# Expert matrices fetched as one 16 KB piece per partition, and the two halves of the down product computed side by side

## The reference, cut to what matters

```
def expert_block(args):
    xe, e = args
    return (jax.nn.silu(xe @ w_gate[e]) * (xe @ w_up[e])) @ w_down[e]
...
'w_gate': nrm(ks[16], (DEPTH, N_EXPERTS, d, f), d ** -0.5),      # d = 1024, f = 512
'w_up': nrm(ks[17], (DEPTH, N_EXPERTS, d, f), d ** -0.5),
'w_down': nrm(ks[18], (DEPTH, N_EXPERTS, f, d), f ** -0.5),
```

## Time and profile before

| | |
|---|---|
| median of 3 runs | 2983.72 us (2981.38 to 2986.08) |
| the profiled execution, its own time | 2976.64 us |
| its span, first to last instruction | 2974.8 us |
| PE busy | 2399.9 us, 81% |
| DVE busy | 1747.3 us, 59% |
| ACT busy | 1194.0 us, 40% |
| mean granted TensorE clock | 0.891 of full speed |
| expert stage of layer 0, of layer 1 | about 1548 to 2087 us, about 2399 to 2941 us of the span |

### The profile page before, as it was taken

How to read it: one execution, slowest core, us unless ns; L and a number is a source line. 1 busy time by engine, 2 the same in 40 slices (tenths; PEclk the granted TensorE clock), 3 DMA queues, 4 the chain that set the end, 5 groups by cost and what they waited for, 6 DMA issues and landing times. The chain is left out here.

```text
span 2974.8 us, 30862 instructions
## 1 busy us (share of the span) xinstructions
PE 2399.9 (81%) x11408; PEld 1674.4 (56%) x11408; DVE 1747.3 (59%) x2142; ACT 1194.0 (40%) x1399; POOL 347.7 (12%) x431
## 2 busy tenths in 40 slices
PE   5779789996798998877739999999267569999995
PEld 4557677875676776644625555554155445555552
DVE  3646545445473545476347767776547357777674
ACT  2223244332232442244026566565214146566662
POOL 0100000100000001000122111121110122111211
PEclk9879999997898998888759999999579679999997
DMA  8235465550545643500349999998610479999993
GB/s 294 86 124 205 141 197 179 177 198 29 207 165 171 212 173 126 143 1 1 128 172 367 384 389 384 384 385 301 208 28 1 151 246 387 389 390 385 382 380 145
DMA packets 315905, 655.44 MB, mean 220 GB/s; under 512 B 18192, under 2 KB 63840, under 8 KB 315040
## 3 DMA queue, kind: packets, MB, share of 16 engines
q1 hardware_dynamic: 296272, 612.13, 57.6%
q0 software_dynamic: 18288, 38.72, 4.1%
q10 hardware_dynamic: 1248, 3.25, 0.3%
HBM read 653.70 MB, written 21.31 MB: 227 GB/s over the span
## 5 line engine op out<-in xcount | busy, mean ns | idle before, releaser
L554 PE MATMUL bank<-sb_ring_rounded,sb_hT_rounded 128*128 128x512 f32 x2864 | 767.4, 404 | 38.8 <-DVE sb_ring_rounded L1486 11.3
L554 PEld LDWEIGHTS bank<-sb_ring_rounded,sb_hT_rounded 128*128 128x128 f32 x2864 | 554.2, 195 | 163.4 <-issue 14.7
L1486 DVE TENSOR_TENSOR sb_ring_rounded<-sb_ring,sb_ring_rounded 128x2048 fp32r<-128x2048 f32 (+1 forms) x150 | 332.7, 2259 | 242.0 <-ACT sb_ring_rounded L1103 241.7
L1022 PE MATMUL bank<-sb_ring,sb_arena 128*64 128x512 f32 x1024 | 453.1, 595 | 1.8 <-DVE sb_arena L2044 1.8
L2035 DVE TENSOR_TENSOR sb_ring_rounded<-sb_ring,sb_hT_rounded 128x2048 fp32r<-128x2048 f32 x128 | 287.6, 2288 | 247.2 <-ACT sb_hT_rounded L1362 245.5
L1103 ACT ACTIVATE sb_ring_rounded<-sb_ring 128x2048 fp32r<-128x2048 f32 (+1 forms) x150 | 275.2, 1884 | 325.8 <-PE bank L554 146.7
L1000 PE MATMUL bank<-sb_ring_rounded,sb_arena_rounded 128*128 128x512 f32 x1024 | 405.2, 396 | 0.0
L554 PE MATMUL bank<-sb_ring_rounded,sb_arena_rounded 128*128 128x512 f32 x976 | 299.4, 394 | 2.0 <-DVE sb_arena_rounded L1474 1.0
L1022 PEld LDWEIGHTS bank<-sb_ring,sb_arena 128*64 128x64 f32 x1024 | 135.0, 137 | 268.6 <-issue 264.5
L1362 ACT ACTIVATE sb_hT_rounded<-sb_ring 128x2048 fp32r<-128x2048 f32 x128 | 237.3, 1901 | 84.2 <-DMA sb_ring<-in_w_gate 84.2
L1000 PE MATMUL bank<-sb_hT_rounded,sb_arena_rounded 128*128 128x512 f32 x512 | 212.8, 416 | 68.4 <-DVE sb_arena_rounded L2039 68.4
(11 more groups left out here) (292 smaller groups left out, 2847.3 us busy)
## 6 DMA issues: line engine op xcount, KB each, us to landing
sb_ring<-in_w_gate SPq DMA_DIRECT2D x64, 2048.0 KB, 20.2
sb_ring<-in_w_up SPq DMA_DIRECT2D x64, 2048.0 KB, 23.2
sb_ring<-in_w_down SPq DMA_DIRECT2D x64, 2048.0 KB, 20.3
sb_ring<-in_w_ada SPq DMA_DIRECT2D x48, 1024.0 KB, 8.4
sb_ring<-in_ffn_w_gu SPq DMA_DIRECT2D x44, 1024.0 KB, 7.9
sb_ring<-in_xa_w_kv SPq DMA_DIRECT2D x16, 1024.0 KB, 10.8
sb_ring<-in_ffn_w_down SPq DMA_DIRECT2D x16, 1024.0 KB, 6.6
sb_ring<-in_od_w_in SPq DMA_DIRECT2D x12, 1024.0 KB, 8.7
```

Of the source, the lines that this page charges most:

```text
L554: ins = pe.matmul(bank[b][0:rows, :], rnd(x), rnd(w[:, k, :]), start=start and k == k0 and q == 0, stop=stop and k == k1 - 1 and q == len( ...
L1022: ins = pe.matmul(bank[S0 + n][0:ROWS, :], mactT[:, j, k, :], w[:, k, n * NB:(n + 1) * NB], start=k == 0, stop=k == 3)
L1486: dve.tensor_tensor(rnd(w), w, whole(high_of(n)[:, k0:k1, :]), ALU.subtract).then_inc(*c.up(s["w_lo"]))
```

## The change

The fetches, the two groups of transposes and the down product change together. A partition p of a gate or up slot held rows p, 128+p, 256+p and so on of the matrix, eight pieces of 2 KB; of a down slot, rows p, 128+p, 256+p and 384+p, four pieces of 4 KB. Now it holds rows 8p to 8p+7 (of the down matrix 4p to 4p+3), which lie side by side in DRAM. To match, the transposes take every 8th column of the tokens from k on (every 4th of the activations), where they took 128 adjacent ones. The down product alternates between its halves, and the hi half goes to PSUM partitions 64 to 127.

```
-                    src = src.rearrange("o (k p) n -> p (o k) n", p=P)
+                    src = src.rearrange("o (p k) n -> p (o k) n", p=P)
...
-                        ins = pe.transpose(bank[T0 + j][:, k * ROWS:(k + 1) * ROWS], mx[0:ROWS, j, k * P:(k + 1) * P], ident[0:ROWS, 0:ROWS])
+                        ins = pe.transpose(bank[T0 + j][:, k * ROWS:(k + 1) * ROWS], mx[0:ROWS, j, k:D:KD], ident[0:ROWS, 0:ROWS])
...
-                        ins = pe.transpose(bank[2 * j][:, k * ROWS:(k + 1) * ROWS], mact[0:ROWS, j, k * P:(k + 1) * P], ident[0:ROWS, 0:ROWS])
+                        ins = pe.transpose(bank[2 * j][:, k * ROWS:(k + 1) * ROWS], mact[0:ROWS, j, k:EXP_H:4], ident[0:ROWS, 0:ROWS])
...
-                    for n, part in enumerate(("lo", "hi")):
-
+
+                    for part in ("lo", "hi"):
                         since(pe, m[f"y_{part}"], e)
-                        for k in range(4):
-                            ins = pe.matmul(bank[S0 + n][0:ROWS, :], mactT[:, j, k, :], w[:, k, n * NB:(n + 1) * NB], start=k == 0, stop=k == 3)
-                        ins.then_inc(m[f"pe_y_{part}"], 1)
+                    for k in range(4):
+                        for n, part in enumerate(("lo", "hi")):
+                            ins = pe.matmul(bank[S0 + n][n * ROWS:(n + 1) * ROWS, :], mactT[:, j, k, :], w[:, k, n * NB:(n + 1) * NB],
+                                            start=k == 0, stop=k == 3)
+                            if k == 3:
+                                ins.then_inc(m[f"pe_y_{part}"], 1)
...
-                    dve.tensor_copy(my[0:ROWS, j, NB:2 * NB], bank[S1][0:ROWS, :]).then_inc(m["y_hi"], 1)
+                    dve.tensor_copy(my[0:ROWS, j, NB:2 * NB], bank[S1][ROWS:P, :]).then_inc(m["y_hi"], 1)
```

## The result

The changed kernel takes 2909.88 us (median of 4 runs, 2906.74 to 2913.15), the kernel before 2984.05 us (4 runs, 2981.38 to 2986.08). The ratio is 0.9752, with a 95% interval of 0.9735 to 0.9769: 74 us less, where 92 were forecast.

The account below looks back on a forecast made before the run. The DMA queue was taken to bound the expert steps, with other loops close behind. Savings of 45 + 40 us in the layers' steps and 13 at the ends, 98, less 6 given back, made 92: 2892 us, range 2868 to 2932.

Parts of the forecast that it names:

- What bound the kernel before: Expert stages: the DMA queue ends last in each step, 17.05 us in layer 0 and 16.68 us in layer 1.
- The cross-check: ACT's waits for the gate matrix, 46 + 38 us, plus 13 us at the layers' ends: 97 us.
- Part 1, the rate: Expert fetches in 16 KB pieces: 428 GB/s, steps of 15.3 and 15.0 us, saving 45 + 40 us with the floor.
- the 6 us given back: Expert steps: 0.1 us a step subtracted from the saving, for two loops within 0.3 us tied by six slots.
- Part 2: Down product's halves side by side: 3.24 us less a product, on the path only at layer ends, 13 us in all.
- Part 3: Twelve stepped transposes a step: costed at nothing, covered by PE's 2.7 us of slack and 0.48 us free at the four.
- the doubling: Stepped transposes: at most twice as long, 0.12 us each, and hidden; a rival with slow ones, 0.43 us, had 4%.
- The floor: Loop of DVE and ACT in an expert step: 15.0 us, which the change doesn't shorten.
- The clock rival: PE's clock falls in one step of six, 3.4 us each: 34 us back, 2926 us; chance 6%.
- The rivals of the rate: Expert transfers stay at 385 GB/s: 2971 us, 6%; or 16 KB pieces fall to 350 GB/s: 3085 us, 5%.
- of the overlap: Rival: no overlap in the down product, PE's chain of 15.77 us is the step; saves 53, 2931 us; 7%.
- the prediction's price for each packet: DMA transfers: 0.018 us for each packet plus 0.0358 us a KB, so 0.604 us for a 16 KB piece.

Follow-up runs that it names:

- e4: The kernel before with three quarters of the gate and up work left out, all transfers kept in 2 and 4 KB pieces: 2956.71 us.
- e2: The kernel before with only the down product side by side, fetches and transposes unchanged: 2964.17 us, ratio 0.9957.
- e3: The changed kernel with three quarters of the gate and up work left out, all transfers kept in long pieces: 2872.06 us.
- e5: The changed kernel with two float32 matmuls, read by nobody, in PE's wait for DVE after each down product: 2905.2 us, ratio 0.976.
- e12: e5 with POOL's gathers and scatters cut to 8 of 64 rows, all work on the matrices still done: 2873.01 us.
- e1: The kernel before with only the new fetch layout and stepped transposes, down product unchanged: 2952.04 us, ratio 0.9908.
- e8: The changed kernel with each expert matrix fetched by two transfers of 8 KB pieces: 2909.8 us, ratio 0.9767.

## Why the prediction was right, and where it was off

Sign, mechanism and range were right: 2909.88 us lies within 2868 to 2932. Point by point:

- **What bound the kernel before.** Right: with three quarters of the gate and up work gone, the short pieces still gave 382 GB/s (e4), and the side by side product alone didn't shorten the steps (e2). The cross-check (46 + 38 + 13 = 97 us) came near by luck: it left out ACT's waits for the up matrix, as long again, 42.9 us in layer 0 and 34.6 in layer 1:

```profile
ACT sb_hb_rounded L1362 <- DMA sb_ring<-in_w_up: 42.9, 25, 2.7
```

- **Part 1, the rate.** This is the term that was mis-sized. "The cautious end is the rate really seen, 428 GB/s" gave steps of 15.3 and 15.0 us. Measured are 408 and 412 GB/s in the stages, and 412 and 416 with little other work (e3). With the prediction's own bytes that is 6.55 / 0.408 = 16.05 and 6.43 / 0.412 = 15.6 us; the steps came out at 15.91 and 15.54. The queue's packets came to 27 a step and engine (10757 in 400 us), where the prediction counted 24. The 428 had been read in 8 us of one queue that had the engines to itself, and was carried over to 500 us of matrices with POOL's rows beside them. The steps gave 45 - 27.0 = 18 us less than the sum had in layer 0 and 40 - 28.5 = 11.5 us less in layer 1, 29.5 in all; of the 11.5, up to 5 may be the clock's dips (e5). Against it stand the 6 us given back for two loops close to each other, which were not on top of that, and 1.4 us more at the ends and elsewhere: 92 - 29.5 + 6 + 1.4 = 69.9 us.
- **Part 2.** Right. Sixteen records take 3.65 us (forecast 3.84, before 7.08), PE's wait for DVE is 2.25 us a step in layer 0 (forecast 2.7), the ends gave 13.2 us (forecast 13; alone, 13.2).
- **Part 3, "I cost them at nothing".** The cover held, the price didn't. Four transposes take 0.69 us in place of 0.46, eight 1.09 in place of 0.71. The loads behind them went from 138 ns to 201 ns with a step of 8 columns, and to 215 ns with a step of 4. The eight before, then the eight and the four after (ns min/median/max):

```profile
L988 PEld LDWEIGHTS bank<-sb_cst,sb_arena x248: 135/138/142, 1547.8 to 2053.7; 64*128 64x128 f32 x124
```

```profile
L988 PEld LDWEIGHTS bank<-sb_cst,sb_arena x248: 182/201/203, 1548.0 to 2027.7; 64*128 64x128 f32 x124
...
L1010 PEld LDWEIGHTS bank<-sb_cst,sb_arena x128: 192/215/216, 1560.9 to 2047.5; 64*128 64x128 f32 x128
```

The Trainium skill ("SBUF — State Buffer", "Door 1: The DMA port swizzle") has reads at full rate only with two hits in each 16-byte line. The trace agrees that one hit costs; it costs 1.5 times, and the doubling was the prediction's own estimate of the most. In a step without a dip the price is covered: the four end at 1654.36 and DVE, done with another copy, starts on their result at 1654.84, 0.48 us later, as before (1777.42 and 1777.90); and e2, whose transposes have no step, has the same 15.14 us in its shortest steps. DVE's waits for the four (17.4 us in 12 times) come with the clock's dips and not with the stepped reads: e12 has these reads and no dip in its steps, and shows two such waits in layer 0, of 4.1 us together. In e1, without the shorter down product, the 0.61 us lie on the path of every step.
- **The floor.** 15.0 us was forecast, 15.14 is seen in e12 in every step.
- **The clock rival** (given 6%). The dips came, and oftener and cheaper than the rival had them: 1.15 us in 11 of 30 steps, where it had 3.4 us in one step of six. The trace of the changed kernel read by itself would lay 13 us a layer on them. e5 takes them away and the time stays within the noise. They are real and, at this rate of transfers, free in layer 0 and nearly so in layer 1 (at most 5 us).
- **The rivals of the rate** (385 GB/s, 350 GB/s) and of the overlap fell. The Trainium skill's page "DMA: Bandwidth & Descriptors", section "Bandwidth", which the prediction read as a bound of 358 GB/s for any core, also says that this is the share of each when both cores of a pair stream, and gives 425 GB/s as measured for a core alone. This program runs on one core, and 408 to 420 GB/s over hundreds of us agree with the second reading, not with a bound of 358.

What stays open: why the total stops at 416 to 420 GB/s, with few rows from POOL, and not at the 428 of those 8 us; that the memory read differs (results just written there, weights here) was not tried. What makes the short pieces slower is open too: e8 rules out the prediction's price for each packet above 8 KB, but no run has pieces between 4 and 8 KB, or short pieces that lie side by side in DRAM. Also open is whether in layer 1, where the dips and the queue each ask for about 15.5 us a step, taking POOL's rows away while leaving the dips would gain anything.

## What to carry to other kernels

Where several loops are within a few per cent of each other, the parts of a change must be priced together: here they gave 26 and 14 us alone and 74 together, since each uncovers a loop that the other shortens. A rate for a stage of hundreds of us is to be read from a stretch with the same traffic beside it, not from the fastest few us in the trace. With slots filled ahead, a wait list without a DMA in it doesn't say that the transfers are off the path: compare the bytes that a step needs, over the rate that the same transfers reach with most of the other work left out, with the mean step. The rate of the stage itself says nothing, since it follows the step.

## What the runs showed of the hardware

- Float32 matmuls on two column ranges ran fully side by side: sixteen records of 512 columns in 3.65 us, where they took 7.08 us on one.
- Pieces of 8 and of 16 KB went at the same rate, 407 to 414 GB/s; pieces of 2 and 4 KB at 382 to 386, with the DMA engines fully busy each time.
- SP's own time at its fetches changed too. The transfer of an up matrix held its queue for 8.1 us before (median), and for 0.33 us now. The issues from the two traces (1600 to 2000 us; ns min/median/max), before and after:

```profile
L474 SPq DMA_DIRECT2D sb_ring<-in_w_up x23: 2292/8082/8653, 1613.1 to 1985.8; - x23
```

```profile
L474 SPq DMA_DIRECT2D sb_ring<-in_w_up x25: 332/333/333, 1612.1 to 1994.8; - x25
```

- A stepped read made PE's weight loads 1.5 times as long, not twice: 138 to 201 ns (8 columns) and 215 ns (4 columns); the wider step was the faster one.
- The granted clock fell to its lower level in 11 of 30 steps of a layer, in the step shown after PE had waited 2.11 us for DVE, and had risen again by 1668.4, while PE worked on. In these stretches it is 0.95 and 0.96 in the mean. In the kernel before, where PE's wait in the step shown is 1.37 us, it was 1.00, and in e5, with fillers in that wait, 0.99 and 1.00.
